# Scan, attention and merge of a mix layer: three blocks and their order of items made into one block

## What is computed

```python
o_a = gqa_block_attention(q, k, v)              # softmax(q k * scale) v, 4 query heads, 2 kv heads
y   = y_f + y_b + d_skip * xh                   # state-space scan, both directions, 4 heads
o_b = rms_norm(y * silu(z), g_norm)
w   = softmax(q1 k1 * scale + bias) - lam * softmax(q2 k2 * scale + bias)   # 4 heads
o_c = rms_norm(w @ v, g_diff) * (1 - lam_init)  # differential attention
o_d = spatial_gating(...)
gates  = sigmoid(h @ w_branch_gate)             # 1024 -> 4 x 1024
merged = sum(gates * branches @ w_branch)
x = x + merged @ w_out
```

## Time and profile before

| | |
|---|---|
| median of 3 runs | 3546.79 us (3544.7 to 3547.58) |
| the profiled execution | 3549.96 us, span 3548.1 us |
| mean granted TensorE clock | 0.99 |
| TensorE busy (PE) | 3444.6 us, 97% |
| TensorE weight loads (PEld) | 2393.9 us, 67% |
| VectorE busy (DVE) | 1681.2 us, 47% |
| ScalarE busy (ACT) | 1182.0 us, 33% |
| HBM read | 616.52 MB |

### The profile page before, as it was taken

The page is one execution under the profiler, slowest core; times in us unless marked ns, Lnnn a source line. Parts: engine busy times, 40 slices in busy tenths (PEclk is TensorE's granted clock), DMA queues, the critical chain, the costliest instruction groups (busy, mean ns, idle before and its releaser), DMA issues. The chain is left out here.

```text
span 3548.1 us, 44551 instructions
## 1 busy us (share of the span) xinstructions
PE 3444.6 (97%) x17232; PEld 2393.9 (67%) x17232; DVE 1681.2 (47%) x2844; ACT 1182.0 (33%) x1876; POOL 0.2 (0%) x4
## 2 busy tenths in 40 slices
PE   8999999999999999999999999999998999999998
PEld 6788888866788887757886444437756887444436
DVE  6665545468665538575334111127667334111116
ACT  6632224147522224375332000024356333000003
POOL 0000000000000000000000000000000000000000
PEclk9999999999999999999999999999999999999998
DMA  4222233220122221211236999992211225999992
GB/s 158 98 95 95 95 101 100 78 98 2 60 95 95 100 95 57 75 61 64 96 130 246 411 420 419 420 390 69 88 65 42 96 93 221 393 420 420 419 420 102
DMA packets 120448, 620.84 MB, mean 175 GB/s; under 512 B 13597, under 2 KB 14117, under 8 KB 73961
## 3 DMA queue, kind: packets, MB, share of 16 engines
q1 hardware_dynamic: 120296, 618.75, 45.7%
HBM read 616.52 MB, written 4.28 MB: 175 GB/s over the span
## 5 line engine op out<-in xcount | busy, mean ns | idle before, releaser
L457 PE MATMUL PS<-WK_r,RING_r 128*128 128x512 f32 x1312 | 511.7, 390 | 0.0
L455 PE MATMUL PS<-WK_r 128*128 128x512 f32 x856 | 336.8, 393 | 0.0
L456 PE MATMUL PS<-HT_r,WK_r 128*128 128x512 f32 x856 | 333.8, 390 | 0.0
L457 PE MATMUL PS<-AR_r,RING_r 128*128 128x512 f32 x768 | 300.6, 391 | 0.0
L457 PEld LDWEIGHTS PS<-WK_r,RING_r 128*128 128x128 f32 x1312 | 245.4, 187 | 53.8
L449 ACT ACTIVATE WK_r<-RING 128x1024 fp32r<-128x1024 f32 x126 | 133.1, 1058 | 383.1 <-PE PS L457 374.5
L455 PE MATMUL PS<-AR_r,RING_r 128*128 128x512 f32 x640 | 251.4, 393 | 9.2 <-DVE HT_r L452 9.2
L456 PE MATMUL PS<-HT_r,RING_r 128*128 128x512 f32 (+1 forms) x624 | 245.3, 393 | 0.0
L452 DVE TENSOR_TENSOR RING_r<-RING,WK_r 128x1024 fp32r<-128x1024 f32 x126 | 154.1, 1224 | 181.1 <-ACT WK_r L449 181.1
L452 DVE TENSOR_TENSOR RING_r<-RING,RING_r 128x1280 fp32r<-128x1280 f32 (+1 forms) x80 | 113.0, 1413 | 247.6 <-ACT RING_r L449 247.6
L452 DVE TENSOR_TENSOR RING_r<-RING,EXTRA_r 128x1024 fp32r<-128x1024 f32 (+1 forms) x138 | 170.4, 1236 | 105.8 <-ACT EXTRA_r L449 105.8
(11 more groups left out here) (485 smaller groups left out, 6067.8 us busy)
## 6 DMA issues: line engine op xcount, KB each, us to landing
AR<-moe SPq DMA_DIRECT2D x144, 1024.0 KB, 23.3
RING<-moe SPq DMA_DIRECT2D x120, 1024.0 KB, 21.3
EXTRA<-moe SPq DMA_DIRECT2D x72, 1024.0 KB, 20.3
RING<-ff_in SPq DMA_DIRECT2D x96, 512.0 KB, 3.4
RING<-branch SPq DMA_DIRECT2D x64, 640.0 KB, 3.8
RING<-ff_out SPq DMA_DIRECT2D x48, 512.0 KB, 3.4
WK<-moe SPq DMA_DIRECT2D x24, 1024.0 KB, 24.8
RING<-mix_in SPq DMA_DIRECT2D x44, 512.0 KB, 3.5
```

The source lines that it names most:

```text
L455: nc.tensor.matmul(out, r(w_high), r(x_high), start=start, stop=False)
L456: nc.tensor.matmul(out, r(w_high), r(x_low), start=False, stop=False)
L457: return nc.tensor.matmul(out, r(w_low), r(x_high), start=False, stop=stop)
```

## The change

`ssm_scan`, `attention` and `merge` become one function `mixers`, whose two stages lie in one block with the router. The first stage holds scan items 0 to 9, with the masks and the normed x. The second holds scan items 10 to 15, the attention and the merge. The masks of heads 2 and 3 lie in SBUF (EXTRA) and no longer in PSUM, and the bias goes to EXTRA; its load is issued in the first stage behind the row sums and ahead of the branch weights.

Scores 0 and 1 are issued behind scan items 12 and 13 on TensorE, shifts 0 and 1 behind items 13 and 14 on VectorE. The 16 differential items come first, the 8 grouped ones behind them. The fillers (9 + 12 + 6 in the scan, 14 in the attention) are gone. The steps of the two norms are spread over the items: squares of the scan branch behind item 1 on ScalarE, its token sums behind item 3 on TensorE, its mean behind item 5 on VectorE; head squares behind items 9 and 17, both head sums behind item 18, one square root for both norms behind item 22. The rounding of the merge's inputs runs behind items 2 to 14 on ScalarE, and their low parts behind items 17 to 20 and 22 on VectorE; the first two weights are rounded behind items 11 and 12. TensorE starts the merge with the 16 matmuls of the first unit that need no low part of x, then spreads both norms, then goes on; the first trip of the loop is written out.

```diff
     def att_pe(pe, s, items, then, before, lead):
-        score(0)
-        score(1)
-        keep_busy(6, 14)
+        lead(score)
...
-        shift(0)
+        lead(shift)
         for n in range(len(items)):
-            if n + 1 < len(items):
+            if n and n + 1 < len(items):
                 shift(n + 1)
             dve.wait_ge(s["exped"], 2 * (n + 1))
             step(nc.vector.reciprocal(RC[n % 3], RS[n % 3]))
             for ins in items[n].weigh(step, SB[n % 3], RC[n % 3], CO[n % 3]):
                 ins.then_inc(s["weighed"], 1)
+            then(n)
...
-        MR = [[wk(2 * h + d) if h < 2 else bank(2 * (h - 2) + d) for d in range(2)] for h in range(4)]
+        MR = [[wk(2 * h + d) if h < 2 else extra(7 + 2 * (h - 2) + d) for d in range(2)] for h in range(4)]
...
+    BIAS = extra(0, 7).rearrange("p (h m) -> p h m", h=4)
+        items = difference_items() + grouped_items()
+        GROUPED = 4 * TT
...
+            def _(pe):
+                def lead(score):
+                    for n in range(CUT, len(SCAN)):
+                        scan_pe(pe, s, n)
+                        if n in (12, 13):
+                            score(n - 12)
+                    pe.wait_ge(s["gated"], 1)
+                def then(n):
+                    if n == 3:
+                        token_sums(pe, s, "squared", 2, [wk(10), wk(11)], 7)
+                    if n == GROUPED - 2:
+                        pe.wait_ge(s["mean"], 1)
+                    if n == GROUPED + 2:
+                        pe.wait_ge(s["hn_copied"], 2)
+                        head_sums(0)
+                        head_sums(1)
+                att_pe(pe, s, items, then, before, lead)
...
+                for k in range(KD):
+                    pe.wait_ge(s["x_high"], k + 1)
+                    nc.tensor.matmul(bank(0), r(WH[0][:, tile(k)]), r(XH[k]), start=(k == 0), stop=False)
+                pe.wait_ge(s["w_split"], 1)
+                for k in range(KD):
+                    nc.tensor.matmul(bank(0), r(slot(w, 0)[:, tile(k)]), r(XH[k]), start=False, stop=False)
+                pe.wait_ge(s["exped"], 2 * len(items))
+                pe.wait_ge(s["inverse"], 1)
...
+            def _(act):
+                def then(n):
+                    if n == 1:
+                        for c in range(2):
+                            act.wait_ge(s["gated"], c + 1)
+                            nc.scalar.activation(wk(10 + c), wk(BR + 2 + c), ACT.Square).then_inc(s["squared"], 1)
+                        act.wait_ge(s["x_normed"], KD)
+                    if n in (9, 17):
+                        square(n // 8 - 1)
+                    elif 2 <= n < 11:
+                        x_high(n - 2 if n < 9 else n - 3)
+                    if n in (11, 12):
+                        weight_high(act, s, w, n - 11, n - 11, 0, WH, s["gates_in"])
+                    if n in (13, 14):
+                        x_high(n + 1)
+                    if n == GROUPED + TT + 1:
+                        output(0)
+                    if n == GROUPED + TT + 2:
+                        act.wait_ge(s["o_out"], 1)
+                        x_high(KD)
+                        act.wait_ge(s["mean"], 1)
+                        act.wait_ge(s["hn_mean"], 1)
+                        nc.scalar.activation(ROOTS, ROOTS, ACT.Sqrt).then_inc(s["root"], 1)
...
+            def _(dve):
+                def lead(shift):
+                    dve.wait_ge(s["bias"], 16)
+                    for n in range(CUT, len(SCAN)):
+                        scan_dve(dve, s, n)
+                        if n == CUT:
+                            gated(0)
+                        if n in (13, 14):
+                            shift(n - 13)
+                def then(n):
+                    if n == 0:
+                        gated(1)
+                    if n == 5:
+                        dve.wait_ge(s["summed"], 1)
+                        v.tensor_scalar(R4, bank(7, 0, TT), 1.0 / BW, EPS, ALU.mult, ALU.add).then_inc(s["mean"], 1)
+                    if GROUPED + 1 <= n <= GROUPED + 4:
+                        x_low(2 * (n - GROUPED) - 2)
+                        x_low(2 * (n - GROUPED) - 1)
+                    if n == GROUPED + TT:
+                        dve.wait_ge(s["hn_summed"], 2)
...
+                    if n == GROUPED + TT + 1:
+                        weight_low(dve, s, w, 0, 0, WH)
+                    if n == GROUPED + TT + 2:
+                        x_low(KD)
+                        x_low(KD + 1)
...
     for l in range(LAYERS):
-        ssm_scan(l)
-        attention(l)
         with joined():
-            route(l, merge(l))
+            route(l, mixers(l))
```

More of the change, by code:

```diff
@@ L1164, in shifted, with att_pe @@
         return sum(1 if x.bias is None else 2 for x in items[0:n + 1])
-    def att_pe(pe, s, items, then=lambda n: None, before=lambda n: None):
+    def att_pe(pe, s, items, then, before, lead):
         def score(n):
@@ L1206, in att_pe, with att_act @@
         values(len(items) - 1)
[L1208 removed]
+    def att_act(act, s, items, then):
         def exps(n):
[L1210 to L1215, removed]
+            act.wait_ge(s["maxed"], shifted(items, n))
+            if items[n].bias is None and n >= 3:
+                act.wait_ge(s["turned"], n - 2)
             for m in range(2):
@@ L1238, in att_act, with att_dve @@
             then(n)
-    def att_dve(dve, s, step, items):
+    def att_dve(dve, s, step, items, then, lead):
         def shift(n):
@@ L2244, in _ @@
                     sp.wait_ge(s[f"rows{h}"], 16)
+                sp.wait_ge(s["bias"], 16)
             @block.tensor
             def _(pe):
[L2248 to L2264, removed]
@@ L2435, in merge @@
         WH = [RING[:, 6], RING[:, 7]]
-        X = [HT[:, k] for k in range(KD)] + [wk(BR + k) for k in range(2 * NB)]
+        XS = [HT[:, k] for k in range(KD)] + [wk(BR + k) for k in range(2 * NB)]
         XH = [ar(8 + k) for k in range(KD + 2 * NB)]
-        with stage("gates_in gates free dve_step o_scaled" + SPLIT + OUT) as (block, s):
-            out = Output(s, mix_out[l], arc, lambda eng, u: eng.wait_ge(s["dve_step"], 3 * u + 3),
+        X_ORDER = [0, 1, 2, 3, 4, 5, 6, 7, 14, 15, 8, 9, 10, 11, 12, 13]
+        with stage("gated squared summed mean spread inverse root normed o_out dve_step merge_step gates_in gates free o_scaled"
+                   + ATT + HEAD_NORM + SPLIT + OUT) as (block, s):
+            s = {**scanned, **s}
+            out = Output(s, mix_out[l], arc, lambda eng, u: eng.wait_ge(s["merge_step"], 3 * u + 3),
                          [wk(8 + 2 * b, 2) for b in range(2)], [ar(16 + b) for b in range(2)])
@@ L2474, in unit @@
+                for n in range(CUT, len(SCAN)):
+                    scan_act(act, s, n)
+                att_act(act, s, items, then)
+                output(1)
+                act.wait_ge(s["o_out"], 2)
+                x_high(KD + 1)
+                for k in range(4):
+                    act.wait_ge(s["normed"], k + 1)
+                    x_high(KD + 2 + k)
                 def unit(i, j, ahead=True):
@@ new lines, in _ @@
+                dve.sem_inc(s["free"], NB)
+                att_dve(dve, s, step, items, then, lead)
+                dve.wait_ge(s["root"], 1)
+                v.reciprocal(ROOTS, ROOTS).then_inc(s["inverse"], 1)
+                weight_low(dve, s, w, 1, 1, WH)
+                x_low(KD + 2)
+                x_low(KD + 3)
+                dve.wait_ge(s["spread"], 1)
+                for c in range(2):
+                    v.scalar_tensor_tensor(out=wk(BR + 2 + c), in0=wk(BR + 2 + c), scalar=par("ssm_g", 2 * l + c),
+                                           in1=bank(2), op0=ALU.mult, op1=ALU.mult).then_inc(s["normed"], 1)
@@ L2503, in unit @@
+                for c, b in ((0, 3), (1, 7)):
+                    dve.wait_ge(s["spread"], c + 2)
+                    dve.wait_ge(s["hn_copied"], c + 1)
+                    v.tensor_tensor(wk(BR + 4 + c), wk(BR + 4 + c), bank(b), ALU.mult).then_inc(s["normed"], 1)
+                for n in range(KD + 4, 2 * KD):
+                    x_low(n)
+                merged = Steps(dve, s["merge_step"])
                 def unit(i, j, ahead=True):
```

297 lines of the change are left out of this document (146 added, 151 removed).

## The result

The changed kernel takes 3525.22 us (3520.45 to 3530.16, four runs) beside 3547.18 of the kernel before (3544.7 to 3550.06, four runs): ratio 0.9937, 95% interval 0.9925 to 0.9949. It is 22.0 us faster where 31 were forecast. 3525.2 lies in the range, 0.8 us inside its slow end.

What follows compares the result with a forecast made beforehand. TensorE, busy 97%, was taken as the bound, with VectorE pacing differential items. Per layer 21.8 us go and 2.7, 3.0 and 0.7 return: 15.5, 31 for both, 3549.96 to 3519.0 profiled, median 3516; range 3509 to 3526.

Steps and rivals of the forecast that it cites:

- both tails: Stretches ending scan and attention, mostly fillers, norm steps and waiting on TensorE: 9.6 us each per layer, to be removed.
- the cold merge start: First 5.3 us of the merge at clock 0.51 after 4.58 us without work: 2.6 us lost per layer, to be removed.
- spreads in the merge: Both norms' spreads, moved from the tails behind the merge's first 16 matmuls on TensorE: 3.0 us back per layer.
- Cover fails: Rival: ScalarE or VectorE too full under the items, added work pushes them; 4 to 5.5 us per layer, 3524 to 3527; chance 0.2.
- own signs of being wrong: Differential mean item above 3.0, clock 0.5 between scan and merge, VectorE waiting for bias, or first merge unit stopping for inputs.
- The lead: Scan items 10 to 15 with first scores and shifts among them: last scan product 2.7 us later, bounds 1.3 and 4.
- The differential items: First 16 attention items, paced by VectorE at 2.86 us each, with ScalarE's roundings fitting under them except for 0.3 us.
- the low parts: VectorE's rounding remainders, two of 0.61 us in each of four grouped items, making those 3.6 us where 3.1 was the pace.
- the table load: ScalarE's load for the square root, 1.28 us ahead of the last copy; about 0.8 us felt, no drain.
- The grouped stretch: Last eight attention items, from item 15 weighed at 2669.5 to last values at 2699.3; bounds 1.7 less, 2 more.
- The clock falls in the handover: Rival: unfilled TensorE waits between scan and attention halve the clock, 2.6 us per fall, one or two per layer; chance 0.12.
- Slower than before: Rival: clock falls between scan and attention and stays halved through the attention; 3643 us; chance 0.03.

Runs made afterwards that it cites:

- fillers and split head sums: Changed kernel plus ten filler matmuls in two handover waits, and the two groups of head sums one item apart: 3517.55 us, ratio 0.9915.
- late roundings: Kernel with ten fillers, head sums apart and token sums spread, plus all merge input roundings and low parts moved behind the last attention item: 3521.26 us.
- head sums apart: Changed kernel with the two groups of head sums behind successive items, no fillers (also called split head sums): 3527.14 us, ratio 0.9944.
- fillers and the sums spread: Changed kernel with ten handover fillers, head sums apart, and token sums four at a time behind items 3 to 6: 3515.55 us.
- the tail and the seven fillers: Spread-sums kernel, square root behind ScalarE's last copy, last three low parts behind VectorE's last item, only seven fillers before second transposes: 3512.75 us.

## Why the prediction was right or wrong

**Right:** the sign, what goes away (both tails, the cold merge start), and the size of nearly every term that comes back. Measured in the changed kernel's second layer and put in the frame of the kernel before:

| | forecast | measured | step's own error |
|---|---|---|---|
| last scan product ends | 2622.6 | 2623.2 | +0.6 |
| item 1 weighed | 2627.1 | 2627.6 | -0.1 |
| item 15 weighed | 2669.5 | 2673.8 | +3.8 |
| last values end | 2699.3 | 2705.0 | +1.4 |
| spreads in the merge | 3.0 | 3.3 | +0.3 |

The last row is the time from the merge's first matmul to its last multiplication, 221.7 us, less the 221.0 of before without its 2.6 for the cold start. The step from 2622.6 to 2627.1 in the prediction adds up only if it starts where VectorE ends, some 1.3 before the last product's end, which it doesn't say. The two steps that are off by more than 1 are the two with the half clock. Where no fall came, both together are right: 107.7 us against 107.8 in the kernel with fillers and split head sums.

**The range** was met, but by luck. Its slow end of 3526 stood for "Cover fails", which did not happen, and the same kernel on the next chip took 3527.58, outside it. Of the prediction's own signs of being wrong one came true in every profile of the changed kernel, a clock of 0.5 between scan and merge. A second came true for a cause that it did not name: from item 1 to item 15 the mean item took 3.3 us (2627.6 to 2673.8, 14 items), above 3.0, but by the token sums and the clock and not by ScalarE.

**The lead** was 3.3 and not 2.7; it shows as the 2.35 us for which VectorE waits for score 0, and stays in the bounds. **The differential items** at 2.86, the low parts at 3.53 against 3.6 and the table load at 0.64 against 0.8 came as forecast. The grouped stretch had the right length, but not because VectorE paced it alone: with the low parts gone it took as long (late roundings). No drain shows behind the table load: it starts as the rounding before it ends, the root starts 1.29 us after it and the copy 0.13 after that. The Trainium skill ("ScalarE: Activation LUTs", What ACT_TABLE_LOAD costs) gives about 1.28 us for the load, which these rows bear out, and with a drain 2.66 in all, which they don't. Nor did the bias come late.

**Wrong** is one step, the weighing of the rival "The clock falls in the handover": a chance of 0.12. The prediction named the place and even the waits (0.9 and 1.7 us forecast, 0.99 and 1.77 measured) and set them aside because of one row: in the earlier trace rows a stretch with TensorE busy 1.47 of 3.00 us kept the full clock. What the chip showed is 1.83 of 3.60 busy with clock 1.00, and the fall right behind it; it came at this place in both layers of both profiled executions of the changed kernel, and in every other layer in which the wait of 1.77 us stood open. A row at full clock tells that the clock had not fallen yet, and not that such a stretch is safe. The forecast was thus a sum without falls, and the kernel as changed does not run without them. The Trainium skill, "TensorE: Matmul & The Clock Gate", Part 1, has the throttled state as the default, which activity releases. The runs agree with the direction: with seven matmuls in the wait, the clock stayed at 1.00 there.

**The price** of a fall was taken from the cold merge start, 2.6 us, and is 3.0 at the handover (109.6 against 106.6, some 7 us at half clock), for another reason than there. In the merge the matmuls simply take twice as long for 5.3 us. In the items, VectorE's 2.86 is the pace until TensorE's 2.65 us per item become 5.0; two slow items lose some 2 us each, and part comes back through what VectorE has ready by then. Two layers had a handover fall of some 10 us; they lie 4.1 and 4.4 above 107.7 once 2.8 for a fall behind the token sums (head sums apart, first layer) or 1.3 for one behind the head sums (changed kernel, second layer) is taken off. The rival "Slower than before" took the right mechanism with a fall that lasts through the attention; it lasts some 7 and 10 us in the first profile, and 3.4 us in the second layer of the second one, so that most of the gain stays.

**Not seen ahead** were the falls behind bunches of small matmuls. The trace of before gave no sign of them: its 8 in 1.05 us and its 16 in 1.95 us, between fillers, had no fall behind them. Of 16 in a row the changed kernel has two bunches per layer. Behind the head sums a fall costs 1.3 (112.3 against 111.0), behind the token sums 2.8, when it comes. At full clock all of them together were costed right.

**Cover fails** (0.2) is refuted, although 3525.2 lies in its interval of 3524 to 3527, as in the clock rival's of 3521 to 3527: the items didn't slow where the roundings lay under them. By the number alone the wrong rival would have been confirmed. What was covered is worth 1.8 us per layer in the traces.

The 9 us then: at full clock the changed order, with fillers and the sums spread, measures 3515.55 where 3516 was forecast, and 3525 to 3528 with the clock as it falls. In the profiled execution the sum closes: of 31 forecast, 20.6 came in the two layers, and the merge starts 4.6 and 5.7 later than in the layer without a fall, 10.3 together. The handover's two falls make 7.5 to 8.9 us in the medians. What the bunches cost in the median was not told from the noise; the traces price each of their falls. The runs that were not profiled say the same by their mean clock: over the 15 of the three kernels without fillers at the handover it goes from 0.991, with 3520 and 3521 us, to 0.986, with 3535 and 3538, though falls elsewhere in the program have a part in that. The best kernels here, with the tail and the seven fillers, take 3513 us, 12 below the changed kernel and 34 to 36 below the one before.

## What to carry to other kernels

When a reordering opens a wait on TensorE in a loop that is nearly balanced between engines, cost it twice: the wait itself, and the stretch behind it at half the clock, in which TensorE's share of each item doubles and it becomes the bound. Before fillers are taken out with a block boundary, ask which new wait takes the boundary's place; seven matmuls in a wait that is there anyway cost nothing and were worth 7.5 us here. The fillers that the kernel before had at the start of its attention were worth nothing that could be measured, so place them by what a trace shows. And spread sums with one column over several items, a few matmuls at a time, even where the engine has the room for all at once: here that took them from a fall in 5 layers of 10 to none in 12. When work is moved away as a test of what it costs, ask what else fills the same time: neither the low parts nor the head sums alone set the length of the grouped items.

## What the runs showed of the hardware

A fall is partly a matter of chance: with the same code and a wait of 2.32 us it came in one layer and not in the other, and the runs of the kernels without any filler at the handover (the changed one, split head sums) spread by 9 to 16 us, those of the kernels in whose profiles no fall came, but for the late roundings, by 2 to 5. So a single profile says where the clock can fall, not how often it does.

A bunch of 16 matmuls with one or two columns shows as 1.95 us of busy TensorE with other work right before and behind it, and in 7 of 16 cases the granted clock was 0.50 soon after. Four such matmuls at a time (0.6 us), or eight (1.05) between the work of the items, never had a fall behind them here; the eight at the end of the attention in the kernel before without its 14 fillers, followed by a wait of 1.34 us, had one in one layer of two.
